# State groups on four quarters of TensorE in a fused layer: backward side exchanged, work moved from GpSimd to ScalarE

## The reference

```python
def s5_scan(uf, b_re, b_im, lam_re, lam_im, log_dt, h0, reverse):
    ab_re, ab_im, f_re, f_im = s5_discretise(lam_re, lam_im, log_dt)
    bu_re = jnp.einsum('btgp,gnp->btgn', uf, b_re.astype(F32))
    bu_im = jnp.einsum('btgp,gnp->btgn', uf, b_im.astype(F32))
    bu_re, bu_im = cmul(f_re, f_im, bu_re, bu_im)
    ...
    _, _, h_re, h_im = lax.associative_scan(s5_combine, (a_re, a_im, bu_re, bu_im),
                                            reverse=reverse, axis=1)
    return h_re, h_im

def trunk_layer(x, cvec, p, rope=None, ctx=None):
    sh1, sc1, g1, sh2, sc2, g2 = modulation(cvec, p['w_mod'], p['b_mod'])
    h = modulate(x, p['norm1'], sh1, sc1)
    u, c_q, c_kv, k_rope = jnp.split(h @ p['w_in'], IN_SPLITS, axis=-1)
    ssm_out, ssm_state = s5_mixer(u, p, None if ctx is None else ctx[2])
    ...
    attn = attend(q, k, v)
    mix = jnp.concatenate([ssm_out, attn], axis=-1) @ p['w_out']
    x = x + g1 * mix
    h2 = modulate(x, p['norm2'], sh2, sc2)
    x = x + g2 * peer(h2, p['w_query'], p['sub_keys'], p['u_table'], p['v_table'])
```

## Time and profile before

| | us |
|---|---|
| median of 3 runs | 841.61 |
| the profiled execution | 841.02 |
| its span, first to last instruction | 839.2 |
| TensorE busy | 707.3 |
| VectorE busy | 591.4 |
| GpSimd busy | 377.2 |
| ScalarE busy | 334.6 |

### The profile page before, as it was taken

How to read it: one execution, slowest core, us unless ns; L and a number is a source line. 1 busy time by engine, 2 the same in 40 slices (tenths; PEclk the granted TensorE clock), 3 DMA queues, 4 the chain that set the end, 5 groups by cost and what they waited for, 6 DMA issues and landing times. The chain is left out here.

```text
span 839.2 us, 10338 instructions
## 1 busy us (share of the span) xinstructions
PE 707.3 (84%) x3385; PEld 352.9 (42%) x3385; DVE 591.4 (70%) x1284; ACT 334.6 (40%) x995; POOL 377.2 (45%) x335
## 2 busy tenths in 40 slices
PE   3899999999978988899869787777877877877784
PEld 0586666656434455677524232323322222322221
DVE  7979623677995658958898856887687578744544
ACT  3423351345466324433344433353334333433331
POOL 3628900244535453444465544446444444455500
PEclk9999999999999999999999999998999999999999
DMA  9956697989999999999999999999999999999992
GB/s 349 419 205 230 224 378 267 351 316 406 419 422 371 422 424 368 422 421 422 387 418 423 422 422 422 422 423 421 422 422 424 421 422 422 422 422 422 422 423 93
DMA packets 50270, 321.74 MB, mean 383 GB/s; under 512 B 9948, under 2 KB 10652, under 8 KB 12200
## 3 DMA queue, kind: packets, MB, share of 16 engines
q0 software_dynamic: 36864, 268.45, 77.6%
q1 hardware_dynamic: 12984, 52.44, 16.3%
q10 hardware_dynamic: 368, 0.18, 0.1%
HBM read 318.77 MB, written 1.23 MB: 381 GB/s over the span
## 5 line engine op out<-in xcount | busy, mean ns | idle before, releaser
L845 PE MATMUL psum<-mem 128*128 128x512 f32 x868 | 429.1, 626 | 95.4 <-ACT mem L1232 95.0
L1507 POOL DMA_INDIRECT mem<-uv_table,small x232 | 279.1, 1203 | 292.4 <-PE psum L845 226.9
L1857 DVE CUSTOM_DVE_ANT_0 mem<-mem,h 128x1024 f32<-128x1024 f32 x232 | 282.6, 1225 | 148.4 <-DMA mem<-uv_table,small 143.3
L845 PEld LDWEIGHTS psum<-mem 128*128 128x128 f32 x868 | 156.6, 195 | 337.0 <-ACT mem L1232 205.4
L1221 ACT ACTIVATE small<-small 128x1 f32<-128x1 f32 x252 | 50.9, 202 | 282.2 <-DVE small L1857 279.4
L1232 ACT ACTIVATE mem<-consts,small 128x128 f32<-128x128 f32 x238 | 95.6, 402 | 7.9
L1226 ACT ACTIVATE small<-small 128x1 f32<-128x1 f32 x256 | 75.4, 294 | 26.3 <-DVEq L1850 3.0
L792 PEld LDWEIGHTS psum<-hT,mem 128*128 128x128 f32 x352 | 42.3, 193 | 11.3 <-issue 7.7
L1507 POOL DMA_INDIRECT spare_page<-uv_table,small x24 | 28.3, 1178 | 40.9 <-PE psum L845 26.7
L1422 POOL TENSOR_SCALAR small<-small 128x1 f32<-128x1 f32 (+1 forms) x9 | 4.6, 514 | 92.0 <-DVE small L1887 44.7
L792 PE MATMUL psum<-hT,mem 128*128 128x128 f32 x352 | 42.4, 276 | 3.4 <-DMA mem<-w_query 3.4
(11 more groups left out here) (239 smaller groups left out, 731.9 us busy)
## 6 DMA issues: line engine op xcount, KB each, us to landing
mem<-w_mod SPq DMA_DIRECT2D x24, 1024.0 KB, 9.6
mem<-w_query SPq DMA_DIRECT2D x6, 1024.0 KB, 9.2
mem<-w_out SPq DMA_DIRECT2D x4, 1024.0 KB, 7.2
mem<-uv_table,small POOLq DMA_INDIRECT x232, 25.8
mem<-w_in_u SPq DMA_DIRECT2D x2, 1024.0 KB, 14.7
late<-w_query SPq DMA_DIRECT2D x2, 1024.0 KB, 9.6
mem<-w_in_qkv SPq DMA_DIRECT2D x2, 1008.0 KB, 12.5
mem<-w_ukv SPq DMA_DIRECT2D x1, 1024.0 KB, 8.3
```

What stands on the lines that cost most here:

```text
L845: mm = pe.matmul(bank(f"acc_{g}_{half}"), diag[:, pick % DEEP, :], row_of(pick)[:, D + 512 * half:D + 512 * half + 512], start=first, stop ...
L1507: pool.indirect_dma_start(row_of(pick), None, uv_table, bass.IndirectOffsetOnAxis(ap=idx[:, pick:pick + 1] if pick else first_idx, axis=0) ...
L1857: dve.tensor_tensor_reduce(out=row[:, 0:D], in0=row[:, 0:D], in1=h[:, pick // PICKS, :], scale=1.0, scalar=0.0, op0=ALU.mult, op1=ALU.add, ...
```

## The change

- **Groups exchanged.** In the backward direction the two groups of a pair change sides: group e has its backward states in the other half of the partitions (`by_unit`, `by_state`, and the copy of the final states). `s5_in(u)` and `input_weights(c)` loop over d inside j, and their 32 products go to the tile positions (0, 0), (64, 64), (0, 64), (64, 0) in turn, forward into one bank, backward into the other. `s5_products` reads real and imaginary halves of both banks. `y_carried(u)` is cut in `y_carried(u, 0)` at the diagonal positions and `y_carried(u, 1)` at the others, 16 products each, the second behind a wait for the first (`forward_done`).
- **To ScalarE.** The decays of units 0 and 1, the 8 copies of `x0` and the initial states (`first_states`) leave GpSimd's list for ScalarE's.
- **Output powers.** `spare` moves to `spare_page`; of the second half of `ypow` one multiplication now follows `s5_products(0)`, and the last operation follows `s5_turns(0)`. `s5_products(3)` goes ahead of `s5_scans(2)`. `ysb` moves to `spare_page` too, and ScalarE's wait for all `kernel_windows` goes.
- **Orders.** TensorE's list from `s5_in(1)` to `pair_step("a", 0)` is rewritten, and SP's: `inputs_to_chunks(3)`, `mod1.1` and `mod1.2` go ahead of `uq` and `ukv`.

```diff
+        spare = spare_page[:, :].rearrange("p (a k q) -> p a k q", a=DT, k=STEP)
+        sparer = spare_page[:, :].rearrange("p (a q k) -> p a q k", a=DT, k=STEP)
...
+        ysb = spare_page[:, 0:512].rearrange("p (b j n) -> p b j n", b=2, j=4)
...
-            for c in range(3):
+            for c in range(NC):
                 inputs_to_chunks(c)
+            load("mod1.1")
+            load("mod1.2")
             sp.wait_ge(coef_used, 1)
             load("uq")
             sp.dma_start(page(0)[:, 1344:1728], w_uq[:, 1920:2304]).then_inc(uq_tail_in, 16)
             load("ukv")
-            inputs_to_chunks(3)
-            for n in range(ORDER["mod1.1"], ORDER["mod1.4"]):
-                load(PAGES[n][0])
+            load("mod1.3")
             for c in range(NC):
                 kernel_windows(c)
                 load(f"mod1.{4 + c}")
...
+                outs = [start(f"W_{c}_{d}") for d in range(2)]
...
+                    for j in range(4):
+                        for d in range(2):
+                            at_ = 256 * r + 64 * j
+                            for e in range(2):
+                                es, hs = side_of(e), side_of(e ^ d)
+                                mm = pe.matmul(outs[d][es, at_:at_ + 64], xrow[hs, r, 8 * c + 4 * d + j, :, :].rearrange("p q k -> p (q k)"),
+                                               ident[hs, hs], start=True, stop=True, tile_position=(hs.start, es.start))
+                            if r == 1 and j == 3:
+                                finish(mm, f"W_{c}_{d}")
...
-                pe.wait_ge(x0_ready, 1)
+                pe.wait_ge(x0_ready, 8)
...
                 for r in range(2):
-                    for a in range(8):
-                        d, j = a // 4, a % 4
-                        for e in range(2):
-                            es = slice(64 * e, 64 * e + 64)
-                            mm = pe.matmul(psum[es, r, 64 * a:64 * a + 64], win[es, u, r, a, :],
-                                           chunks(ut[es, u, j, :].rearrange("p (g n) -> p g n", g=G), d),
-                                           start=True, stop=True, tile_position=(64 * e, 64 * e))
+                    for j in range(4):
+                        for d in range(2):
+                            at_ = 256 * r + 64 * j
+                            for e in range(2):
+                                es, hs = side_of(e), side_of(e ^ d)
+                                mm = pe.matmul(psum[hs, d, at_:at_ + 64], win[es, u, r, 4 * d + j, :],
+                                               chunks(ut[es, u, j, :].rearrange("p (g n) -> p g n", g=G), d),
+                                               start=True, stop=True, tile_position=(es.start, hs.start))
...
-            def y_carried(u):
-                pe.wait_ge(sum_ready, 2 * u + 2)
+            def y_carried(u, d):
+                if d:
+                    pe.wait_ge(forward_done, u + 1)
+                else:
+                    pe.wait_ge(sum_ready, 2 * u + 2)
...
+                    a = 4 * d + j
+                    for r in range(2):
+                        for e in range(2):
+                            es, hs = side_of(e), side_of(e ^ d)
+                            mm = pe.matmul(out[es, 64 * j:64 * j + 64], ypow[hs, r, 8 * u + a, 1:5, :].rearrange("p k q -> p (k q)"),
+                                           chunks(view(u, r)[hs, a, :, 0:CHUNKS], d),
+                                           start=False, stop=j == 3 and d == 1 and r == 1, tile_position=(hs.start, es.start))
+                mm.then_inc(y_ready if d else forward_done, 1)
...
+            s5_in(1)
             input_weights(2)
+            input_weights(3)
             latents(0, (0, 1))
-            s5_in(1)
-            input_weights(3)
-            latents(0, (2, 3))
+            s5_in(2)
+            latents(0, (2, 3, 4, 5, 6, 7))
             quad_step(1, 0)
-            s5_in(2)
-            latents(0, (4, 5))
+            s5_in(3)
             kernels()
-            latents(0, (6, 7))
             quad_step(1, 1)
-            s5_in(3)
             quad_step(1, 2)
+            latents_turned(0)
             y_local(0)
-            y_carried(0)
+            y_carried(0, 0)
+            attention_queries(0, 0)
+            y_carried(0, 1)
+            y_local(1)
+            y_carried(1, 0)
             quad_step(1, 3)
+            y_carried(1, 1)
             pe.wait_ge(bu_used, NC)
-            latents_turned(0)
-            y_local(1)
-            quad_step(1, 4)
-            attention_queries(0, 0)
             attention_queries(0, 1)
-            y_carried(1)
-            quad_step(1, 5)
-            attention_keys(0, 0, "kv")
             y_spread(0)
             y_spread(1)
+            attention_keys(0, 0, "kv")
+            quad_step(1, 4)
             queries_turned(0)
             keys_turned(0, 0)
-            quad_step(1, 6)
             y_local(2)
-            y_carried(2)
+            y_carried(2, 0)
+            quad_step(1, 5)
+            y_carried(2, 1)
             attention_scores(0, 0)
             attention_scores(0, 1)
+            y_local(3)
+            y_carried(3, 0)
+            quad_step(1, 6)
+            y_carried(3, 1)
             y_spread(2)
-            y_local(3)
-            y_carried(3)
             quad_step(1, 7)
             y_spread(3)
             pair_step("a", 0)
...
+            def first_states(u):
+                if u >= 2:
+                    act.wait_ge(bu_ready, (2, 4)[u - 2])
+                for r in range(2):
+                    act.copy(view(u, 2 * r)[:, :, :, 0], h0_sb[:, r, 8 * u:8 * u + 8, :]).then_inc(h0_ready, 1)
...
+            act.wait_ge(mag_ready, 1)
+            act.wait_ge(ones_ready, 1)
+            decays(0)
...
+            decays(1)
+            first_states(0)
+            first_states(1)
...
+            first_states(2)
+            act.wait_ge(x0_zeroed, 1)
...
+                        act.copy(x0z[es, d, r, :, :, 16 * (e ^ d):16 * (e ^ d) + 16], xz[es, d, r, :, :, 3 - 3 * d, :]).then_inc(x0_ready, 1)
             decays(2)
+            act.wait_ge(x0_ready, 8)
+            latent_squares(0)
             kernels_evac()
-            decays(3)
-            latent_squares(0)
             latents_scaled(0)
             latents_evac(0)
-            for q in range(2):
-                query_evac(0, q)
+            query_evac(0, 0)
+            first_states(3)
+            decays(3)
+            y_evac(0)
+            y_evac(1)
+            query_evac(0, 1)
             for q in range(2):
                 wait_emptied(act, f"q_0_{q}")
             act.sem_inc(q_ready, 1)
-            for c in range(NC):
-                act.wait_ge(toep_in[c], 4 * 16)
-            y_evac(0)
-            y_evac(1)
             act.wait_ge(ckv_ready, 1)
...
-            pool.wait_ge(mag_ready, 1)
-            for u in range(2):
-                pool.tensor_tensor(dec[:, u, :, :], ones0[:, :].unsqueeze(1).to_broadcast([P, 8, 2 * SL]),
-                                   rad4[:, 8 * u:8 * u + 8].unsqueeze(2).to_broadcast([P, 8, 2 * SL]), ALU.mult).then_inc(rad4_ready, 1)
-            pool.wait_ge(xpow_ready, 1)
...
-            pool.wait_ge(x0_ready, 1)
-
             def s5_sums(u):
-                if u == 0:
-                    pool.wait_ge(ypow_ready, 2)
-                if u == 2:
-                    pool.wait_ge(bu_ready, 2)
-                if u == 3:
-                    pool.wait_ge(bu_ready, 4)
-                for r in range(2):
-                    step(pool.tensor_copy(view(u, 2 * r)[:, :, :, 0], h0_sb[:, r, 8 * u:8 * u + 8, :]))
                 for r, op in ((0, ALU.add), (1, ALU.subtract)):
                     pool.wait_ge(prod_ready, 4 * u + 2 * r + 2)
...
-            tt(spare, mat(cm, 0), lag_im, ALU.mult)
-            dve.scalar_tensor_tensor(yb_, yb_, -1.0, spare, ALU.mult, ALU.subtract).then_inc(ypow_ready, 1)
-            dve.wait_ge(ypow_ready, 2)
-            dve.sem_inc(coef_used, 1)
...
-                if u < 2:
-                    dve.wait_ge(rad4_ready, u + 1)
-                else:
-                    dve.wait_ge(dec_ready, 8 * (u - 1))
+                dve.wait_ge(dec_ready, 8 * (u + 1))
+                dve.wait_ge(h0_ready, 2 * u + 2)
...
             s5_products(0)
+            tt(spare, mat(cm, 0), lag_im, ALU.mult)
+            dve.sem_inc(coef_used, 1)
             s5_products(1)
             s5_scans(0)
             s5_turns(0)
+            dve.scalar_tensor_tensor(yb_, yb_, -1.0, spare, ALU.mult, ALU.subtract).then_inc(ypow_ready, 1)
+            dve.wait_ge(ypow_ready, 2)
             s5_products(2)
             s5_scans(1)
             s5_turns(1)
+            s5_products(3)
             s5_scans(2)
-            s5_products(3)
             s5_turns(2)
             s5_scans(3)
             s5_turns(3)
...
+    a = np.stack([a[..., 0, :, :, :, :], a[..., 1, :, :, ::-1, :]], axis=n)
...
+    a = np.stack([a[0], a[1, :, :, ::-1]], axis=0)
```

70 lines of the change are left out of this document (27 added, 43 removed).

## The result

| | before | after |
|---|---|---|
| median, us | 841.64 (840.71 to 842.75, 4 runs) | 850.74 (847.40 to 853.57, 4 runs) |
| the profiled execution | 841.02 | 847.40 |
| first gather in it | 153.28 | 159.78 |

The ratio is 1.0106, with a 95% interval of 1.0083 to 1.0129: slower by 9 us. The change does what it says on TensorE, and the start of the gathers still comes 6.5 us later. Three executions of 1009.15, 1176.45 and 2458.91 us (one in the run with the kernels sooner, the others of the kernel before) are in the slow state and left out of the ratios.

The account below looks back on a forecast made before the run. The gathers' start (153.28 us), set by TensorE's list and the mod2a.0 load ending together, was the bound. Gains vanish in waits: 0.0 us change, 839.2 span plus 1.8 is 841.0, 0.6 under the median; forecast 841.6, range 838.6 to 844.4.

Parts of the forecast that it names:

- part 1: s5_in and input_weights on four quarters: 1.03 us a group instead of 2.01; cut y_carried gains nothing.
- Rival A: s5_in and input_weights: quarters do not overlap, groups stay at 2.01 us, 847.1 us in all; chance 0.10.
- part 2: Start, decays off GpSimd: modulation columns 0.7 us earlier, first projection at 36.6; ScalarE's new work costs nothing.
- the 47.2 of the sum: Start of s5_in(0) on TensorE: first projection at 36.6 plus 10.6 us for three projections.
- the first two `input_weights` stand ahead of a wait: Before the first projection: these two groups precede the wait for modulated inputs, so only six of eight lie on the path.
- part 3: From first projection to end of kernels: 34.5 us plus 0.3 waiting for VectorE, ending at 71.4 against 73.16.
- Rival C: VectorE late with s5_products(2) ahead of s5_in(3): last ypow operation takes up to 8.9 us, 847.1 us; chance 0.14.
- part 4: Between kernels and y_local(0): kernel_windows land at 76.4, TensorE's other work ends at 74.2, the gain's first loss.
- It waits 2.2 us: TensorE ahead of y_local(0): idle from 74.2 until kernel_windows land at 76.4.
- part 5: quad_step(1, 6) ends at 102.2; mod2a.0, behind out0.1, lands at 109.8; TensorE waits 4.7 us, starts at 109.95 as before.
- The pair of the earlier trace: Loads mod2a.0 and out1.1: the second landed 7.5 us after the first's issue, the term used for out0.1 and mod2a.0.

Follow-up runs that it names:

- the run with the kernels sooner: On the changed kernel, kernels() ahead of two latents steps and s5_in(3), latents_turned(0) later, ScalarE's kernels copy first: 847.70 us, ratio 1.0068.
- the filler: Overwritten products added to the changed kernel: 8 ahead of input_weights(0), 849.80 us; for the 1.7 us clock cost, 20 ahead of pair_step(a, 0), 848.79 us.
- the second trace: The changed kernel measured once more, unchanged: 849.65 us, ratio 1.0101 to the kernel before.
- load_first: On the changed kernel, the load of mod2a.0 put ahead of out0.1 in SP's queue: 844.74 us, ratio 1.0032.
- mod13_later: On the changed kernel, the 1 MB load of mod1.3 issued behind kernel_windows(0): 850.67 us, ratio 1.0099.
- spread: On the changed kernel, steps of latents placed between s5_in(1), input_weights(2) and input_weights(3), two more between s5_in(3) and kernels(): 851.17 us, ratio 1.0116.

## Why the prediction was wrong

- **Product groups (part 1): right.** 1.09 us for `s5_in`, 1.03 assumed. Rival A is out, and with it, for these groups, the rule of the Trainium skill named there (page "TensorE: Matmul & The Clock Gate", Part 3), by which the prediction would have left the groups at 2.0. `kernels`, which the change does not touch, took 1.8 instead of 2.46. The 0.66 us in `input_weights(3)` was not foreseen.
- **The start (part 2): wrong by 0.9 us in the first trace, and by more where the clock was low.** There `s5_in(0)` came at 48.8 to 51.7, 1.6 to 4.5 us behind the 47.2 of the sum. VectorE takes the columns at 32.61, but the projection started at 37.49, not at 36.6. The last copy into `hT` ended at 36.43 (ScalarE), and before, the projection began 0.37 us behind that copy; here it is 1.06, put down to "issue", at the first of the places above. So some 0.7 us are a stop for which the prediction had no term. And "the first two `input_weights` stand ahead of a wait" was costed at nothing: their saving became idle time, and behind it the clock was low in ten of twelve traces with that gap unfilled (12.0 to 12.2 us for the projection, 10.5 in the other two, behind 2.81 and 2.41 us). In the six with the filler and the two of the kernel before it took 10.4 to 10.7.
- **The end of `kernels` (part 3): right by luck.** 71.9 for 71.4: a start 0.9 us late and the stop of 0.66 against `kernels`, 0.6 us faster, and a wait of 0.3 us that did not come. Rival C did not come: the last of `ypow` took 2.28 us, not 3.4. But the moved multiplication took 3.42 and not 2.3, with GpSimd's sums beside it, so VectorE was done with `s5_products(2)` at 68.7 and not at 67.9; in the second trace TensorE waited 0.87 us for it.
- **The wait for the windows (part 4): this step failed.** "It waits 2.2 us" took only SP's windows as the bound and gave `latents_turned` 0.75 us of work in the gap. They landed at 76.7, near the forecast, but `latents_turned` stood waiting in front of `y_local(0)`, which came at 78.97 and not 76.4: 2.6 us. I had named no queue behind GpSimd's normalisation for it. (To move `latents_turned` alone gained nothing, since the windows landed later in that trace; the run with the kernels sooner took the wait away.) The low clock that followed made the stretch to `quad_step(1, 6)` 26.7 us, not 25.8, so it ended 3.5 us late, at 105.7.
- **The load (part 5): mechanism right, term too small.** TensorE stands still until `mod2a.0` lands, behind `out0.1`; load_first shows it. The pair took 9.0 us from the step's end and not 7.5. The pair of the earlier trace rows had no third load issued half a microsecond behind it; that this is the 1.5 us was not tried. Late end (3.5) and longer landing (1.5) make 4.8 us at `pair_step`, within rounding and the 0.15 us between landing and start.
- **The clock: a term that was missing.** The prediction had TensorE idle for 4.7 us and let it go on at full speed. That costs 1.7 us behind the load, shown by the filler. 4.8 and 1.7 are the 6.5 us of the trace. The median lies another 3.3 us higher: the slow projection can give 1.6 of it, as in the second trace; the rest was not traced run by run, and its cause stays open.

The forecast of no change rested on one thing: that a gain lost in a wait costs nothing more than itself. Here most waits were followed by products at half the speed, which moved the next load's release and with it the end of the next wait.

## What to carry to other kernels

Where TensorE is made faster ahead of a wait, price the idle time and not only the saving: write down, for each gap that the faster products open, what the products behind it would take at the lower clock, and who is released by them. Then look who can work in the gap; here the order of work on three engines, loads put ahead of others, and products that fill 1.9 us together turned 850 us into 839.3. What each is worth alone is shown for the load of `mod2a.0` only (4.9 us).

## What the runs showed of the hardware

- Idle times without a semaphore, 0.2 to 3.2 us long, stand at fixed counts of TensorE's instructions (at the first of them TensorE also waits for `hT`), some 126 passes or twice that apart, and end 2.2 to 2.7 us after a 16 KB packet of an instruction queue starts (39 stops in twenty traces, 30 to 125 us). Not each place has a stop in each trace: the one behind 473 passes is absent from the second trace of the change. Behind 852 passes the stop is 1.2 to 2.1 us in the seven traces with the change's list up to `kernels` and its loads, 0.45 where a 1 MB load was moved away (mod13_later), and none in spread. The Trainium skill, page "Runtime: NRT & Kernel Launch", section "Instruction fetch mechanics", says that instructions are refilled in blocks of 16 KiB, 256 of them, and that the cost of crossing a block is mostly hidden. The traces agree on the size of the block and on the count (252 instructions in 126 passes); with products of 16 to 17 ns a pass the crossing is not hidden. That late instructions are the cause is thus well supported, but was not tried by itself.
- 64x64 products on four quarters in turn take 17 ns a pass; two diagonal positions and then the two others, with the bank changed between, 21 to 23; the diagonal positions alone 31.
- TensorE's granted clock fell to the lower of its levels behind most idle times of 2.2 to 5.8 us, not behind all: it stayed at 1.00 behind 2.81 us in the first trace and 2.41 us in spread. Where products whose result is overwritten stood in such a gap, it stayed up in all seven traces.
